# Other order of updates, squares, row sums and products at the two layer ends of a streaming encoder step

## What is computed

```
h = x + 1/2 * g1 * SwiGLU1(mod(rms(x)))          # d_ff = 2816
h = h + gm * Mixer(mod(rms(h)))
h = h + 1/2 * g2 * SwiGLU2(mod(rms(h)))
y = mod(rms(h))
Mixer: z = xn @ w_in; conv + RG-LRU branch; V -> GeLU -> layernorm -> spatial gating; merged @ w_out
```

## Time and profile before

| | |
|---|---|
| median of 3 runs | 2569.76 us (2568.68 to 2570.29) |
| profiled execution, its own time | 2574.91 us |
| its span in the trace | 2573.2 us |
| PE busy | 2437.8 us, 95% |
| DVE, ACT, POOL busy | 1665.5, 1054.7, 166.9 us |
| granted PE clock, mean | 0.972 of full speed |
| first layer end, last round to V tile 6 | 874 to 970 us |
| second layer end | 2504 us to the end |

### The profile page before, as it was taken

One profiled execution on the slowest core, in us unless ns is written; L12 is line 12 of the kernel. 1 busy time (PEld: TensorE's weight loads), 2 busy tenths in 40 slices (PEclk: granted clock), 3 DMA queues, 4 the chain that ended last, 5 costly groups with the idle time before them and its releaser, 6 DMA issues.

```text
span 2573.2 us, 32028 instructions
## 1 busy us (share of the span) xinstructions
PE 2437.8 (95%) x11514; PEld 2050.1 (80%) x11514; DVE 1665.5 (65%) x2636; ACT 1054.7 (41%) x1817; POOL 166.9 (6%) x199
## 2 busy tenths in 40 slices
PE   7899999999899989999999998968999999989997
PEld 3477777777788767999999998956777788878786
DVE  4977667666566765655566666168667657666675
ACT  2544444444333432433333444125445444433334
POOL 3000000000000000001101110110000000000000
PEclk9899999999999989999999999988999999999997
DMA  9245544556855422421222224023554543496531
GB/s 359 71 150 168 184 156 149 184 167 218 322 221 213 157 91 79 135 61 45 57 61 61 61 65 159 16 106 99 163 162 150 172 143 123 154 351 259 221 131 76
DMA packets 245119, 381.02 MB, mean 148 GB/s; under 512 B 16641, under 2 KB 158137, under 8 KB 243462
## 3 DMA queue, kind: packets, MB, share of 16 engines
q1 hardware_dynamic: 232302, 345.15, 38.5%
q0 software_dynamic: 10240, 33.56, 4.7%
q10 hardware_dynamic: 2456, 0.75, 0.1%
HBM read 262.93 MB, written 116.47 MB: 147 GB/s over the span
## 4 chain that ended last, share of the span: by engine, by line
PE 69%; DVE 16%; DMA 6%; issue 5%; ACT 3%; SPq 1%; DVEq 0%; ACTq 0%; POOL 0%
PE bank L482 20%; PE bank L483 20%; PE bank L484 20%; DVE u_lo L559 3%; DMA h_dram<-stage_lo 3%; DMA wraw<-in_w_ffn_down 2%; PE bank L2552 1%; PE bank L2550 1%; PE bank L2553 1%; DVE stage_lo L1794 1%; DVE wraw L586 1%; PE bank L2461 1%; DVE ada_lo L1809 1%; PE bank L2568 1%; DVE h L1802 1%
## 5 line engine op out<-in xcount | busy, mean ns | idle before, releaser
L482 PE MATMUL bank<-ops,u_hi 128*128 128x512 f32 x1232 | 490.6, 398 | 21.6 <-ACT g L1153 10.9
L559 DVE TENSOR_TENSOR u_lo<-wraw,u_hi 128x512 fp32r<-128x512 f32 (+2 forms) x532 | 317.5, 618 | 287.6 <-ACT u_hi L553 284.8
L483 PE MATMUL bank<-ops,u_hi 128*128 128x512 f32 x1232 | 487.1, 395 | 0.0
L484 PE MATMUL bank<-ops,u_lo 128*128 128x512 f32 x1232 | 485.9, 394 | 0.0
L482 PE MATMUL bank<-xn_hi,w_hi 128*128 128x384 f32 x1152 | 387.9, 337 | 15.7 <-DVE xn_lo L2343 9.7
L553 ACT ACTIVATE u_hi<-wraw 128x512 fp32r<-128x512 f32 (+2 forms) x532 | 289.6, 567 | 261.9 <-PE bank L484 167.7
L483 PE MATMUL bank<-xn_lo,w_hi 128*128 128x384 f32 x1152 | 385.7, 335 | 0.0
L484 PE MATMUL bank<-xn_hi,w_lo 128*128 128x384 f32 x1152 | 385.6, 335 | 0.0
L482 PEld LDWEIGHTS bank<-ops,u_hi 128*128 128x128 f32 x1232 | 235.2, 191 | 85.8 <-ACT g L1153 12.5
L484 PEld LDWEIGHTS bank<-ops,u_lo 128*128 128x128 f32 x1232 | 235.0, 191 | 51.3
L483 PEld LDWEIGHTS bank<-ops,u_hi 128*128 128x128 f32 x1232 | 235.6, 191 | 49.8
(11 more groups left out here) (305 smaller groups left out, 4242.9 us busy)
## 6 DMA issues: line engine op xcount, KB each, us to landing
h_dram<-stage_hi SPq DMA_DIRECT2D x154, 256.0 KB, 2.4
h_dram<-stage_lo SPq DMA_DIRECT2D x154, 256.0 KB, 2.7
ada_raw<-in_w_ada POOLq DMA_DIRECT2D x96, 256.0 KB, 3.1
raw<-in_w_in SPq DMA_DIRECT2D x48, 512.0 KB, 4.7
wraw<-in_w_ffn_gate SPq DMA_DIRECT2D x44, 512.0 KB, 3.8
wraw<-in_w_ffn_up SPq DMA_DIRECT2D x44, 512.0 KB, 4.8
wraw<-in_w_ffn_down SPq DMA_DIRECT2D x48, 384.0 KB, 5.4
x<-x_dram SPq DMA_DIRECT2D x6, 2304.0 KB, 11.9
```

Source lines behind the costliest of these rows:

```text
L482: nc.tensor.matmul(out, hi, mov_hi, start=first, stop=False, skip_group_check=True)
L483: nc.tensor.matmul(out, hi, mov_lo, start=False, stop=False, skip_group_check=True)
L484: return nc.tensor.matmul(out, lo, mov_hi, start=False, stop=last, skip_group_check=True)
L559: nc.vector.tensor_tensor(unit(u_lo, u, n), unit_source(u, n), unit(u_hi, u, n).bitcast(F32), ALU.subtract).then_inc(u_lo_ready, 1)
```

## The change

First layer end (f = 0). `last_of_first` replaces the general round in the last of the eight: PE's order becomes A11, samples, S2, samples, turned rows, A12, S3, turned rows, A22, S1, row sums of half 0, S4 with the spread between its two tiles. Units 12 to 15 lie at places 6 and 7 of the ring. DVE's 14 updates come in the order W0 W1 F0 F1 V0 X0 X1 Y0 Y1 Z0 Z1 S0 S1 V1 (F first snaps, Y the Z banks of S1, V the snaps of A22, S the snaps of S3). All sixteen squares are added by DVE, so that PE's row sums have one source a half. The samples' sum, root and spread come ahead of those of half 1; a copy in SBUF (`factor_copy`) takes the place of the bank that DVE read. V's tiles 4, 5, 6 run as one group, with the GeLU table and tile 0's eviction between ACT's first and second `normalised(1, k)`.

Second layer end (f = 1). `last_of_second`: product order as before except that the turned rows follow the second samples, the second turned rows come ahead of S3, and the samples' sum ahead of S4. Two more squares of half 0 are added by DVE. Updates in the order Y0 Y1 S0 S1 W0 W1 F0 F1 V0 V1 X0 X1 Z0 Z1, then the samples' norm and then the output rows. The samples are finished first.

In round 0 of f = 1 the transposes of the final shift (line 2732), which stood in one piece, are parted: the second four come behind S3, their copy on ACT behind `unit_hi` 5 of the next round.

```diff
-TAIL_SQUARES = ([(c, k, False) for k in range(KH) for c in range(2)]
-                + [(0, 4, True), (0, 6, True), (1, 5, True), (1, 7, True), (0, 5, True), (0, 7, True),
-                   (1, 4, True), (1, 6, True)])
+FFN1_SQUARES = TAIL_SQUARES + [(0, 4, False), (0, 6, False), (0, 5, False), (0, 7, False),
+                               (1, 5, False), (1, 4, False), (1, 6, False), (1, 7, False)]
+FFN2_SQUARES = TAIL_SQUARES + [(0, 4, False), (0, 6, False), (1, 5, True), (1, 7, True), (0, 5, True), (0, 7, True),
+                               (1, 4, True), (1, 6, True)]
+RANK = ((1, 2, 3), (1, 3, 2), (1, 2, 3), (2, 3, 1))
...
+            def half_sums(i, c):
+                pe.wait_ge(xs_written, i + c)
+                last = max(p for p in range(NSQ) if SQUARES[i][p][0] == c)
+                pe.wait_ge(acc_added, added(i, last + 1))
+                pe.wait_ge(squared, i * NSQ + last + 1)
...
+                    if k == KT - 1 and t == 2:
+                        spread(1, 1)
                     v_step(0, t, k)
                 if k == 3:
-                    early_sums(1, 1)
-                    late_sums(1, 1)
+                    sample_sums(1)
                 elif k == 5:
-                    spread(1, 1)
+                    spread(1, 2)
+                elif k == 6:
+                    half_sums(1, 1)
...
-                for t in (4, 5):
+                for t in (4, 5, 6):
+                    if k == 0 and t == 6:
+                        pe.wait_ge(act_evicted, 1)
                     v_step(0, t, k)
```

More of the change, by code:

```diff
@@ L1314, in down @@
                     if not more:
[L1315 removed]
+                        if f == 0:
+                            last_of_first()
+                        else:
+                            last_of_second()
+                        return
                     unit_hi(act, f, g, 12)
                     unit_hi(act, f, g, 13)
[L1318 to L1319 removed]
                     if rho == 0:
@@ L1464, in _ @@
             for half in range(2):
-                for t in range(NT):
+                for t in range(1 - half, NT):
                     m = half * NT + t
@@ L1967, in update, with named, w_part, f_part @@
                           .then_inc(x_written, 1)
+                    names = []
+                    def named(name, tile, c, src):
+                        names.append(name)
+                        assert names == LAST_UPDATES[f][:len(names)]
+                        update(tile, c, src)
+                    def w_part(m):
+                        dve.wait_ge(ffn_mm, done(f, g, E_P2[m]))
+                        named(f"W{m}", (a0, a1)[m], 0, bank[WB[m]][:, :])
+                    def f_part(m):
+                        dve.wait_ge(snapped, snaps(f, g, m + 1))
+                        dve.wait_ge(x_written, last_update(f, f"W{m}"))
+                        named(f"F{m}", (a0, a1)[m], 0, snap_first[:, m, :])
@@ new lines, in v_part, with y_part @@
+                    def v_part(m):
+                        dve.wait_ge(snapped, snaps(f, g, m + 5))
+                        if f"Y{m}" in names:
+                            dve.wait_ge(x_written, last_update(f, f"Y{m}"))
+                        named(f"V{m}", (b0, b1)[m], 1, snap[:, 2, m, :])
+                    def y_part(m):
+                        dve.wait_ge(ffn_mm, done(f, g, E_P5[m]))
+                        if f"V{m}" in names:
+                            dve.wait_ge(x_written, last_update(f, f"V{m}"))
+                        named(f"Y{m}", (b0, b1)[m], 1, bank[ZB[m]][:, :])
@@ L2684, in turn_rows, with shift_turn @@
                         last.then_inc(srow_turned, 1)
+                    def shift_turn(b):
+                        if b == 1:
+                            pe.wait_ge(shift_copied, 1)
+                        for k in range(KH):
+                            last = nc.tensor.transpose(bank[7][:, k * P:(k + 1) * P],
+                                                       prompt_scalar(SHIFTF, 4 * b + k).broadcast_to([P, P]),
+                                                       ident[:, :])
+                        last.then_inc(shift_turned, 1)
```

577 lines of the change are left out of this document (364 added, 213 removed).

## The result

The changed kernel takes 2545.98 us (median of 5 runs, 2540.11 to 2551.10); the kernel before took 2569.76 beside it (2564.43 to 2576.81). The ratio is 0.9909, with a 95% interval of 0.9883 to 0.9934. The forecast was 2547.4.

What follows compares the result with a forecast made beforehand. PE, busy 95%, bounds the kernel, so only its idle time, non-product work and half clock can go. 2569.76 - 15.4 (first end) - 7 (second end), shift transposes 0, gives 2547.4 us; range 2538 to 2556, own range 2543 to 2551.

Steps and rivals of the forecast that it cites:

- The 8.72 us wait and tile 6: First end: PE's wait for tile 0's eviction goes (9.0 us with a transpose), tile 6 no longer at half clock (2.9).
- wait 6: First end: spread of half 1 waits, its reciprocal standing behind three steps of the samples' norm on DVE; 1.6 us.
- Row sums and what follows them: First end: fewer row sums save 5.0 us in half 0, 3.6 in half 1; products at half clock 5.2.
- new falls: First end: the clock falls again at stretches of row sums and idle time; 2.2 us in all, bounds 0 and 8.
- The eight new waits: First end: walking the three new instruction lists against each other gives eight PE waits or added costs, sum 11.2 us.
- Wait 5: First end: row sums of half 1 wait for the last of four squares added on DVE; 1.45 us.
- wait 2: First end: S4's first tile waits for Y0, behind V split 0 and the reciprocal on DVE; 1.9 us.
- wait 4: First end: ACT's root for the samples waits for their sum, delaying `xn_hi` of k = 4, `xn_lo` and PE; 1.65 us.
- wait 1: First end: second samples, now after S2, wait for unit 11's low part, behind ACT's first squares; 1.9 us.
- the prediction's own sign: Both ends: wrong if an unnamed place has a wait over 3 us, or the clock falls elsewhere than at the snap.
- full clock until half 1's sums: Second end, rival: full clock through it until half 1's sums, -15.5 us there, 2538.9 in all; chance 0.22.
- the walk at full clock: Second end: DVE's last row at 2553.4 instead of 2570.05, saving 16.7 us, or 15.5 with a fall in half 1's row sums.

Runs made afterwards that it cites:

- the block of 64: Changed kernel with extra one-column matmuls (32 and 64 records) between V tiles of the second half; tile 7 to the modulation's wait takes 845.56 us for 827.27.

## Why the prediction was right, and where it was not

**First end: -15.4 forecast, -14.65 measured** (12.6 to 16.8 over the pairs of two profiles of before and five of the changed kernel). The size is right, the book under it is not: three entries were of the wrong size and cancelled, so that the number fits so closely is luck.

- *The 8.72 us wait and tile 6* (9.0 + 2.9 = 11.9 "goes"). The step that failed is "GeLU stood behind all of ACT's work for half 1": true, but that work was late because of the norm, which moved too. Undoing GeLU and group costs 1.18; the norm as well, 6.75. The prediction booked the norm's move only as a price (wait 6, 1.6 us), so its entry for the three together was 10.3.
- *Row sums and what follows them* (8.6 + 5.2, less 2.2 of new falls: 11.6). Undoing them costs 8.55: 6.8 of own time at full clock, where 8.6 at the clock they had were booked, and half clock 20.5 instead of 13.6 us.
- *What is left*, the old waits of 2.49 and 1.53 us against the new ones: 3.1 less 9.6, so -6.5 by the book. 8.55 + 6.75 = 15.3 is the 14.65 within the clock's spread, so it comes to about nothing. That is by subtraction; the two were not undone in one run. Read from the rows instead: PE's waits fell from 12.74 to 8.81 us, 64 records less are 6.8, and of the half clock about 20.7 us lay on work before and 11.7 after, 4.5 us; in all an estimate of 15.2.
- *The eight new waits* (11.2): seven have a price, and the profile shows six of them at the places named.

| wait | forecast | after |
|---|---|---|
| 1 unit 11 | 1.9 | 1.77 |
| 2 Y0 | 1.9 | 1.50 |
| 3 Y1 | 1.45 | 1.50 |
| 4 `xn_lo` behind the root | 1.65 | 1.75 |
| 5 half 1's additions | 1.45 | 0 |
| 6 spread of half 1 | 1.6 | 1.20 |
| 7 chain of half 1 | 1.0 | 1.09 |

Sum 8.8. Wait 5 is in no profile of the changed kernel's order: PE came later and DVE was done. The snap's, forecast at 0.93 (1.53 less 0.6), is 1.05 or 1.06 in the four other executions with the same instructions, and gone in the profile of after, where half clock at 884 to 887 held PE back by more than that.

- *The clock*: 2.2 for new falls. The profile of after shows three stretches: one from 901.1, behind wait 2, as forecast, one at wait 4, and one behind wait 1, where none was forecast. In other executions the last is missing behind the same 1.77 us. The bounds 0 to 8 held; a forecast of single falls can't. By the prediction's own sign, a fall at another place than the snap, it was wrong on the clock.

**Second end: -7 forecast, -9.82 in this profile, -7.1 by the median of eight.** The snap's wait of 3.0 us is 2.75. That the clock falls at it is right in this profile, where it is at 0.50 from 2508.7 to 2515.6, but it came back before half 0's row sums and fell a second time in half 1's, where the forecast had it at half until 2549. In six of the eight executions the first fall comes within 1.6 us of that wait's end and in one 5 us behind it. In the profile of the group alone undone it comes only in half 1's row sums, 16 us behind the wait, which is the rival *full clock until half 1's sums*; that execution saves 9.6 us, not 15.5. Taking half of the half clock off each of the eight leaves an estimate of 48.8 to 51.9 us, where the walk at full clock had 48.8, so the walk held and the clock was the open part. Over the eight executions the saving runs from 4.0 to 10.5 us, inside the 0.5 to 15.5 given. By the rows of the two profiles PE's waits fell from 9.8 to 4.5 us, 16 records less are 1.7, and 10.0 us less half clock at most 5.0; no run parts these, so the causes at this end are read and not shown.

**Shift transposes: 0 forecast, about 0 measured** by the run with them together, as far as the clock lets one see. The wait of 4.87 us went and 2.23 and 3.71 came, the second for slot F:

```profile
2275.51 0.47 PE L494 MATMUL bank<-slotE,u_hi 128*128 128x512 f32 x1 [2.23 <-issue]
...
2285.63 0.50 PE L494 MATMUL bank<-slotF,u_hi 128*128 128x512 f32 x1 [3.71 <-DMA slotF<-h_dram]
```

So the wait was covered, as forecast, but not by the weights: DVE's sum was not last, the load of slot F was, and the slots hold the hidden activations (`h_dram`).

**The sum.** -22.4 forecast. Between the two profiles the change is -29.0; 5.15 of it is that the profiled execution of before lay that much above its median, while that of after is its median run. Between the medians it is -23.8, 1.4 us from the forecast. The middle's 4.07 had no entry, and the profile of after is one with little half clock in its second end.

## What to carry to other kernels

Ask of a long wait what the waited-for instruction itself waited for, and which of these the same change moves: two repairs of one wait bring it once. Matmuls of one column cost their own time and the clock of what comes behind; squares summed on an engine that has room, then one block of row sums, were the largest single term at the first end here (8.55 us). When a layer end depends on the clock, forecast it as a spread over executions (here 2 us in one end, 6.5 in the other) and compare variants only over that spread or at equal half clock.

## What was not expected of the hardware

- The clock falls with PE busy throughout: at 943.4 inside 40 one-column records, and in the block of 64.
- The same instructions with the same waits get between 3.4 and 13.6 us of half clock in the first end, and between 14.3 and 27.5 in the second. Stretches at 0.50 came out at 3.4, 6.8, 10.2 or 13.7 us, with the 27.3 us of the kernel before's second end as the longest, apart from those that reach into the idle end of a program. The two ends differ by 2.2 and 6.5 us between executions by it; the times of the five runs lie within 11 us of each other.
- Less half clock does not give back all of it: from 13.6 to 3.4 us in the first end the time fell by 2.15 us and not by 5.1, because the snap's wait of 1.05 us came up in its place, and because 1.9 of the 13.6 us lay in waits. The rest of the difference was not taken apart.
